# Attention and recurrence on one core: another order on ScalarE and TensorE, and one activation table fetched less

## The reference, cut to what matters

```python
z = h @ w_in
q, k, v, zu, zv = jnp.split(z, [D_ATTN, 2 * D_ATTN, 3 * D_ATTN, 3 * D_ATTN + D_SGU], axis=-1)
attn = dilated_attention(q, k, v, rel_bias)     # per branch: exp(q k + bias - max) / sum, times v
sgu = spatial_gating(gelu(zu), gelu(zv), sgu_ln_g, sgu_ln_b, sgu_w, sgu_b)
x = x + rms_norm(jnp.concatenate([attn, sgu], axis=-1) @ w_out, g_post_mix)
...
f = lb + (1.0 - lb) * jax.nn.sigmoid(f_raw)     # recurrence, chunks of 64, 8 heads of 128
o = scores(q, 1 - f, decay of f) @ v + (q * exp(b)) @ S
o = o * rsqrt(mean(o * o) + EPS) * gn_g * silu(g)
```

## Time and profile before

| | us |
|---|---|
| median of 3 runs | 1695.92 (1695.72 to 1695.95) |
| profiled execution | 1694.48 |
| span in it, first to last instruction | 1692.5 |
| PE busy | 1682.7 (99%) |
| DVE, ACT, POOL busy | 1241.9, 816.9, 423.9 |

### The profile page before, as it was taken

The page is one execution under the profiler, slowest core; times in us unless marked ns, Lnnn a source line. Parts: engine busy times, 40 slices in busy tenths (PEclk is TensorE's granted clock), DMA queues, the critical chain, the costliest instruction groups (busy, mean ns, idle before and its releaser), DMA issues.

```text
span 1692.5 us, 29354 instructions
## 1 busy us (share of the span) xinstructions
PE 1682.7 (99%) x9794; PEld 1470.2 (87%) x9794; DVE 1241.9 (73%) x2280; ACT 816.9 (48%) x1429; POOL 423.9 (25%) x217
## 2 busy tenths in 40 slices
PE   9999999999999999999999999999999999999998
PEld 7877788999999888889999998888888889999997
DVE  5655569888887878688688695566675598688685
ACT  5566554333333534654453354565655554353354
POOL 3232320000001498320220203442423320220221
PEclk9999999999999999999999999999999999999999
DMA  7543213233333233233332333231212133342331
GB/s 197 123 95 91 71 56 123 88 100 99 99 99 111 76 119 100 63 104 109 112 111 87 100 101 112 75 100 50 87 62 76 63 111 107 103 128 74 100 113 50
DMA packets 159859, 162.63 MB, mean 96 GB/s; under 512 B 10628, under 2 KB 126968, under 8 KB 159776
## 3 DMA queue, kind: packets, MB, share of 16 engines
q1 hardware_dynamic: 155311, 158.66, 30.8%
q10 hardware_dynamic: 4464, 2.89, 0.6%
HBM read 157.84 MB, written 3.67 MB: 95 GB/s over the span
## 4 chain that ended last, share of the span: by engine, by line
PE 93%; POOL 3%; DVE 1%; ACT 1%; issue 0%; DMA 0%; SPq 0%; DVEq 0%; POOLq 0%; ACTq 0%
PE ps L1967 36%; PE ps L2440 21%; PE ps L2465 10%; PE ps L2319 7%; PE ps L2344 6%; PE ps L1995 2%; PE ps L2547 2%; POOL wlo L995 1%; PE ps L2006 1%; PE ps L2204 1%; PE ps L2223 1%; POOL wsum L1038 1%; POOL first_table L1001 0%; PE ps L2110 0%; PE ps L2116 0%
## 5 line engine op out<-in xcount | busy, mean ns | idle before, releaser
L995 POOL TENSOR_TENSOR wlo<-raw,whi 128x1024 fp32r<-128x1024 f32 x60 | 145.8, 2445 | 588.1 <-ACT whi L1457 292.6
L1967 PE MATMUL ps<-h_hi,wlo 128*128 128x512 f32 x608 | 247.9, 408 | 0.6 <-DVE gv L2875 0.3
L1967 PE MATMUL ps<-h_hi,whi 128*128 128x512 f32 x608 | 238.0, 391 | 0.0
L1967 PE MATMUL ps<-h_lo,whi 128*128 128x512 f32 x608 | 237.6, 391 | 0.0
L1117 ACT ACTIVATE whi<-raw 128x1024 fp32r<-128x1024 f32 x120 | 124.5, 1053 | 113.7 <-PE ps L1967 104.7
L1967 PE MATMUL ps<-m_hi,wlo 128*128 128x512 f32 x384 | 152.7, 398 | 0.2 <-POOL m_lo L1059 0.2
L1967 PE MATMUL ps<-m_hi,whi 128*128 128x512 f32 x384 | 149.7, 390 | 0.0
L1967 PE MATMUL ps<-m_lo,whi 128*128 128x512 f32 x384 | 149.6, 390 | 0.0
L1967 PEld LDWEIGHTS ps<-h_hi,whi 128*128 128x128 f32 x608 | 114.1, 188 | 25.2
L1967 PEld LDWEIGHTS ps<-h_hi,wlo 128*128 128x128 f32 x608 | 114.4, 188 | 23.3 <-issue 1.5
L1967 PEld LDWEIGHTS ps<-h_lo,whi 128*128 128x128 f32 x608 | 114.5, 188 | 21.7 <-issue 1.0
(11 more groups left out here) (516 smaller groups left out, 4936.2 us busy)
## 6 DMA issues: line engine op xcount, KB each, us to landing
raw<-in_ffn_w SPq DMA_DIRECT2D x264, 256.0 KB, 2.9
raw<-in_w_ff SPq DMA_DIRECT2D x128, 256.0 KB, 2.9
raw<-in_hg_w_in SPq DMA_DIRECT2D x64, 256.0 KB, 3.1
raw<-in_w_in SPq DMA_DIRECT2D x40, 256.0 KB, 5.1
raw<-in_cp_w_in SPq DMA_DIRECT2D x24, 256.0 KB, 3.0
raw<-in_w_out SPq DMA_DIRECT2D x16, 256.0 KB, 2.8
raw<-in_cp_w_out SPq DMA_DIRECT2D x16, 256.0 KB, 3.0
raw<-in_hg_w_out SPq DMA_DIRECT2D x16, 256.0 KB, 2.7
```

The costliest lines, as they stand in the source:

```text
L995: pool.tensor_tensor(wlo[:, u % RING, :, :], raw[:, u % RING, :, :], whi[:, u % RING, :, :].bitcast(F32), ALU.subtract).then_inc(unit_lo, 1)
L1967: mm = pe.matmul(ps[:, b, :], wt[:, s, a, m * P:(m + 1) * P], xt[:, kts[a], :], start=starts and a == 0 and i == 0, stop=last)
```

## The change

Four edits. In `attend` of ACT, `weights(1)` goes ahead of the copy of `vtok`, `weights(2)` ahead of the tanh, `weights(5)` and `weights(6)` ahead of `units(1)` and `units(2)`, and `units(0)` moves from behind `turned(0)` to behind `weights(4)`. In `attend` of PE, a dense tile goes between `turn(7)` and the next pair's first scores, and the last tile between the two scores. In pair 0, the dense work's unit 0 takes its tiles in the order v, q, k, u. In the recurrence, the table load that ends `head_gates(0)` goes; since the sigmoid table then still stands, the load that began `head_gates(1)` isn't made either.

```diff
                 act.activation(ug[:, :], ps[:, 3, :], ACT.Copy).then_inc(u_ready, 1)
+                weights(1)
                 act.wait_ge(filled[6], nth("att", "vtok", p))
                 act.activation(vtok[:, :], bank("att", "vtok"), ACT.Copy).then_inc(drained[6], 1)
-                weights(1)
                 if before_it is not None:
                     pair_high(before_it)
                 turned(0)
-                units(0)
+                weights(2)
                 act.wait_ge(drained[3], u_count)
                 act.activation(u_in[:, :], u_in[:, :], ACT.Tanh, scale=GELU_SCALE).then_inc(u_tanh, 1)
-                weights(2)
                 turned(1)
                 weights(3)
                 turned(2)
                 act.wait_ge(sg_ready, 2 * p + 2)
                 act.activation(tile_of(m_hi, 4 + p), ug[:, :], ACT.Copy).then_inc(sg_hi, 1)
                 weights(4)
+                units(0)
                 turned(3)
+                weights(5)
                 units(1)
-                weights(5)
                 turned(4)
+                weights(6)
                 units(2)
-                weights(6)
                 turned(5)
...
-            def head_gates(n, between=None):
+            def head_gates(n, between=None, norm_ahead=True):
...
-                act.preload_act_table_set(LOG_TABLES)
+                if norm_ahead:
+                    act.preload_act_table_set(LOG_TABLES)
...
-            head_gates(0, lambda: split(U_HGIN + 4, 1))
+            head_gates(0, lambda: split(U_HGIN + 4, 1), False)
...
             def attend(p, piece, before_it, following=None,
-                       cuts=(0, 2, 4, 6, 8, 10, 12, 14, 16, 18, 20, 22, 24, 28, 30, 32)):
+                       cuts=(0, 2, 4, 6, 8, 10, 12, 14, 16, 18, 20, 22, 24, 28, 30, 31, 32)):
...
                 turn(7)
+                dense(14)
                 if following is not None:
                     scores(0, following)
-                dense(14)
-                if following is not None:
+                    dense(15)
                     scores(1, following)
...
             def head_units(j0, j, part, turn=0, per=0):
+                behind_mixes = j0 == 4 and j == 0
                 unit(U_QKV + j0, j, h_hi, h_lo, (2 * j, 2 * j + 1), "qkv", up_tags, j == 0, j == 3, turn, per,
-                     use=turn + (j0 // 4 - 1), part=part)
+                     (2, 0, 1, 3) if behind_mixes else (0, 1, 2, 3), use=turn + (j0 // 4 - 1), part=part)
```

## The result

| | before | after |
|---|---|---|
| median of 20 runs, us | 1695.92 (1694.43 to 1697.8) | 1699.12 (1698.57 to 1701.09) |
| span of the profiled execution, us | 1692.5 | 1698.1 |

The changed kernel is slower by 0.19%: ratio 1.0019, 95% interval 1.0013 to 1.0025. The forecast was 1699.3 in 1697.7 to 1701.2.

The account below looks back on a forecast made before the run. PE's queue bounds the kernel (busy 1682.7 of 1692.5 us). The terms 5.7 - 1.3 - 0.6 - 0 - 0.45 = +3.4 us, on the median of 1695.92, give 1699.3 us, range 1697.7 to 1701.2.

Parts of the forecast that it names:

- The moved split: Unit 2's low part at `dense(8)`, pairs 0 to 2: PE waits for POOL, losing 1.91 us each, 5.7 us in all.
- The cover in pair 3: Unit 2 is wanted only behind the last scores, at 186.8; POOL ends at about 185.8, so no loss.
- Exponentials first: In pair 3, PE's three waits for DVE's division, together 1.39 us, mostly go: gain 1.3 us, ends 0.9 to 1.4.
- the third wait: Pair 3's turned tile, 0.32 us lost before: DVE's chain is late next, so some 0.1 us stays.
- The dense tile: Ahead of the next pair's scores, a dense tile covers DVE's last part of q: gain 0.6 us, ends 0 and 0.65.
- The tile order: Unit 0, pair 0: PE starts about 0.5 us sooner, then waits for DVE's first division; gain 0, at most 0.1.
- The table load: Head 0 of the recurrence: without ACT's load the snapshots are ready earlier; gain 0.45 us, ends 0.2 and 0.5.
- the second level: In head 0, DVE's products are late next: next to nothing to spare, but no loss.
- The rival in which the gains fail: In pair 3 the scores still wait on DVE's own chain: 5.7 - 0.9, 1700.7 us; chance 13%.
- the one without waits at `dense(8)`: In pairs 0 to 2 PE never waits for unit 2's low part: only gains, -2.35, 1693.6 us; chance 7%.
- the third: At the three new waits PE's clock falls to 1.2 GHz, adding 3 x 3.7 us: 1710 us; chance 2%.
- waits at 5.0 and gains at 2.6: Ends of the sum's own terms, for the waits at `dense(8)` and all gains; own range stated as 1698.0 to 1700.8.

## Why the prediction was right

It held in its point, its mechanism and in each term. The sum was +3.4 us, the medians differ by 3.2. The single terms were off by 0.03 to 0.13 us, partly against each other.

- **The moved split**: forecast 3 x 1.91, measured 1.86, 1.87 and 1.87 in the trace of the changed kernel, 5.65 in the run that moves only it. The chain was added up from start spacings, which was the right reading: with full durations it would have been 0.2 too long. The cover in pair 3 was there: POOL was done 1.0 us before PE asked, as estimated (185.8 for 186.8).
- **Exponentials first**: forecast 1.3, measured 1.27 in the changed kernel and 1.21 alone. That the third wait would keep 0.1 for DVE's own chain came out at 0.11.
- **The dense tile**: forecast 0.6, measured 0.56 alone.
- **The tile order**: forecast 0, measured 0.01; one wait took the other's place as told.
- **The table load**: forecast 0.45, measured 0.39. The first part was right (0.46); the second level, of which I wrote that there was next to nothing to spare, gave back 0.07.

The rival in which the gains fail fell with the runs of the single edits; the one without waits at `dense(8)` fell with the three rows of PE waiting for POOL; the third did not happen at 1.6 us of idleness but does at 4.06. What the prediction leaned on there is weak: 2.52 us of idleness in the first 16 us left the clock at 1.00 in the trace of before, but in that stretch or right behind it the clock fell in three of the experiments (at 8, 15 and 16 us). That it would hold at the new waits was more guess than reading; the changed kernel and the run with only the split moved show that it did, six waits of 1.60 us in all. Its price was a guess too: 3.7 us a wait, where the three falls that were seen cost 2.6, 2.8 and 1.3.

Two numbers of the prediction don't follow from its own terms. With waits at 5.0 and gains at 2.6 the low end is 1698.3, not 1698.0, and the 5.0 is not derived (three times the stated 1.4 is 4.2). The chances for slower by over 0.2% add up to 0.54, not 0.53. Neither bears on the outcome.

What the sum could not give is the verdict: +3.4 us lay on the bound of 0.2%, and the measured +0.19% (interval 0.13 to 0.25%) lies there as well. That it is slower is sure; whether by over 0.2% is not. The measured terms make 5.60 - 1.27 - 0.56 - 0.39 = 3.4 us. PE's start at the end of head 0 shows 3.7, since it holds the drift of 0.34 between pair 3 and the recurrence; the medians' 3.2 was not followed up.

## What to carry to other kernels

Ahead of moving an instruction on an in-order engine, find who waits for it and count from the last event that pins the engine (here a copy that waits for PE's `turn(2)`): what counts is the chain from there to the consumer, not the slack that the old place had. A call can be moved into the engine's own idle time for nothing (ahead of the waiting copy: 0.01 us in pairs 0 to 2) and cost 1.9 us a pair three steps of the program later. Where one wait is removed, look which one of the next consumer comes due: the tile order took away 0.3 us of idleness and bought nothing.

## What the runs showed of the hardware

- **A DVE instruction with both inputs in SBUF that begins while POOL subtracts ends only behind POOL.** DVE's `m_lo<-ug,m_hi`, with both inputs in SBUF, takes 0.69 us in every run where POOL is idle. Begun 0.47 us after POOL's low part it took 2.46 us in all four pairs, ending 0.54 after POOL did. In the run with the split ahead of turned tile 2, begun 1.82 us into POOL's 2.40, it took 1.13 in pair 3, ending 0.55 after POOL:

```profile
183.25 1.13 DVE L2898 TENSOR_TENSOR m_lo<-ug,m_hi 128x512 fp32r<-128x512 f32 x1 [1.07 <-ACT m_hi L1308]
```

  The kernel before has the same elsewhere. A DVE instruction that takes 0.75 us alone begins 0.57 us into POOL's work, takes 2.39 and ends 0.55 after POOL:

```profile
706.28 2.41 POOL L995 TENSOR_TENSOR wlo<-raw,whi 128x1024 fp32r<-128x1024 f32 x1 [1.77 <-ACT whi L1117]
706.85 2.39 DVE L2672 SCALAR_TENSOR_TENSOR h_lo<-xT,vecs,h_hi 128x512 fp32r<-128x512 f32 x1 [0.16 <-ACT h_hi L1154]
```

  Its DVE instruction `prob<-ps,rden`, which reads PSUM, takes 0.75 us with POOL at work and without. So it is the end of POOL's instruction that counts, and not a shared rate: the tail is 0.54 to 0.55 us whether the overlap was 0.58 or 1.92 us.
- **The price of a fallen clock is more than the wait.** 4.06 us of idleness cost 2.6 us more in pair 0 behind the wait, since PE ran at 1.2 GHz until the clock came back; in pair 1 the same wait cost 2.8 more and in pair 2 1.3. Three waits of 1.60 us left the clock alone.
- **Behind a wait, PE's second matmul comes 0.34 us after the first**, not 0.23, both for POOL (87.55 and 87.89) and for DVE (70.86 and 71.20); an idle time in the waits' list is less than what is lost (1.60 recorded, 1.86 lost).
